# A hybrid encoder layer on eight cores: attention split into producer and consumer pieces, tanh for sigmoid, and a second table started inside the first

## What is computed

```python
h = rms_norm(x, g_mix); q, k, v, x_gate, x_rec = split(h @ w_in)      # 2048 -> 3584
y_attn = windowed_gqa_sink(rope(q), rope(k), v, sink)                # 16 heads of 64, +-128 tokens, sink logit
c = centred_depthwise_conv(x_rec, conv_w, conv_b)                    # 1024 channels
#   rg_lru: r = sigmoid(c @ w_a + b_a); i = sigmoid(c @ w_x + b_x)   # blocks of 64
#           a = exp(-8 r softplus(-lam)); u = sqrt(1 - a*a) * (i * c); h_t = a_t h_{t-1} + u_t
y_lru = gelu(x_gate) * (rg_lru(c, fwd) + rg_lru(c, bwd, reverse=True))
x = x + concat(rms_norm(y_attn), rms_norm(y_lru)) @ w_out
q = rms_norm(x) @ w_pq; s1, s2 = scores of q with 128 + 128 sub-keys per head (8 heads)
gates, eidx = softmax(top 16 of the 16 x 16 best pairs)              # 128 of 16384 experts per token
x = x + sum_e gates_e * gelu(xn . u_emb[e]) * v_emb[e]
out = rms_norm(x, g_final)
```

## Time and profile before

| | us |
|---|---|
| three runs | 6939.51, 6334.04, 7033.96 (median 6939.51) |
| the profiled execution | 6331.23 |
| its span, slowest core (2) | 6329.7 |
| spans of the eight cores | 6294.9 to 6329.7 |
| busy: PE, PEld | 5218.0 (82%), 2522.3 (40%) |
| busy: DVE, ACT, POOL | 3233.7 (51%), 2587.7 (41%), 2413.7 (38%) |

### The profile page before, as it was taken

One profiled execution on the slowest core, in us unless ns is written; L12 is line 12 of the kernel. 1 busy time (PEld: TensorE's weight loads), 2 busy tenths in 40 slices (PEclk: granted clock), 3 DMA queues, 4 the chain that ended last, 5 costly groups with the idle time before them and its releaser, 6 DMA issues.

```text
span 6329.7 us, 87104 instructions; the slowest of 8 cores (6294.9 to 6329.7 us)
## 1 busy us (share of the span) xinstructions
PE 5218.0 (82%) x25339; PEld 2522.3 (40%) x25840; DVE 3233.7 (51%) x6638; ACT 2587.7 (41%) x3722; POOL 2413.7 (38%) x1894
## 2 busy tenths in 40 slices
PE   5895445443687789999999999995799999999994
PEld 2442112111244445555555555442344444444441
DVE  2204556564341876666666666600445555555453
ACT  4523545554222234444444444431344444444443
POOL 1002344344100232222222222300577777777772
PEclk9996566655898999999999999998899999999997
DMA  9731111111973234444444444334554445544542
GB/s 307 236 124 40 41 39 56 43 48 56 268 233 134 80 120 134 146 136 152 137 134 142 139 140 150 128 123 148 181 157 149 152 146 157 157 151 156 155 136 106
DMA packets 388943, 860.25 MB, mean 136 GB/s; under 512 B 95104, under 2 KB 226688, under 8 KB 364928
## 3 DMA queue, kind: packets, MB, share of 16 engines
q1 hardware_dynamic: 374336, 728.82, 37.3%
q0 software_dynamic: 14144, 125.83, 5.0%
HBM read 613.39 MB, written 241.17 MB: 135 GB/s over the span
## 4 chain that ended last, share of the span: by engine, by line
PE 61%; DMA 5%; issue 3%; DVE 3%; ACT 2%; POOL 1%; SPq 1%; DVEq 0%; ACTq 0%; POOLq 0%
PE p_sps L259 28%; PE p_vps L259 25%; PE p_gps L259 4%; PE p_pq L259 2%; DMA s_Gc<-gdn 2%; PE p_pa L259 1%; POOL s_acc L259 1%; PE p_pl L259 1%; SPq L280 1%; DMA s_stfa<-w_out 1%; DMA s_ysqt<-ysq 1%; PE p_psc L259 1%; ACT s_act L259 1%; DVE s_acc L259 1%; DMA gdn<-s_stg 0%
## 5 line engine op out<-in xcount | busy, mean ns | idle before, releaser
L259 PE MATMUL p_sps<-s_xT,s_wq 128*128 128x512 bf16 x7993 | 1822.7, 381 | 28.0 <-ACT s_wq L259 18.3
L259 PE MATMUL p_vps<-s_vr,s_act 128*128 128x512 bf16 x6708 | 1552.7, 383 | 155.2 <-DVE s_acc L259 110.3
L259 POOL TENSOR_TENSOR s_acc<-s_stfa,s_acc 128x512 f32<-128x512 f32 x1024 | 1319.2, 1288 | 501.6 <-ACT s_stfa L259 394.3
L259 PEld LDWEIGHTS p_sps<-s_xT,s_wq 128*128 128x128 bf16 x8192 | 814.8, 100 | 901.1 <-issue 27.1
L259 DVE TENSOR_TENSOR s_acc<-p_vps,s_acc 128x512 f32<-128x512 f32 x1024 | 706.9, 690 | 782.2 <-PE p_vps L259 630.2
L259 PEld LDWEIGHTS p_vps<-s_vr,s_act 128*128 128x128 bf16 x6848 | 673.5, 99 | 981.8 <-issue 194.0
L259 POOL TENSOR_TENSOR s_oA<-s_oA,s_r3T 128x512 bf16<-128x512 bf16 x512 | 552.5, 1081 | 1266.0 <-DVE s_oA L259 1206.1
L259 ACT ACTIVATE s_stfa<-p_vps 128x512 f32<-128x512 f32 x1024 | 556.6, 594 | 951.3 <-POOL s_acc L259 807.7
L259 ACT ACTIVATE s_wq<-p_sps 128x512 bf16<-128x512 f32 x512 | 305.7, 597 | 1102.2 <-PE p_sps L259 1063.0
L259 DVE TENSOR_TENSOR s_oA<-s_iota,s_r3T 128x512 bf16<-128x512 bf16 x512 | 237.0, 463 | 472.1 <-PE p_gps L259 470.0
L259 DVE TENSOR_TENSOR s_act<-s_act,s_Gc 128x1024 bf16<-128x1024 bf16 x256 | 214.6, 838 | 378.9 <-DMA s_Gc<-gdn 378.2
(11 more groups left out here) (164 smaller groups left out, 5242.1 us busy)
## 6 DMA issues: line engine op xcount, KB each, us to landing
s_stfa<-u_t SPq DMA_DIRECT2D x256, 512.0 KB, 4.5
s_stfa<-v_r SPq DMA_DIRECT2D x256, 512.0 KB, 4.7
gdn<-s_stg POOLq DMA_DIRECT2D x32, 2048.0 KB, 8.0
actd<-s_wq SPq DMA_DIRECT2D x128, 512.0 KB, 5.5
s_act<-actd SPq DMA_DIRECT2D x32, 2048.0 KB, 10.0
s_Gc<-gdn SPq DMA_DIRECT2D x128, 512.0 KB, 4.3
s_xt<-x SPq DMA_DIRECT2D x32, 1024.0 KB, 10.7
s_stfa<-w_in SPq DMA_DIRECT2D x52, 512.0 KB, 10.2
```

The costliest lines, as they stand in the source:

```text
L259: pg.op(eng, lambda e: getattr(e, method)(**kw), rd, wr, sig)
```

## The change

Stage B. Every attention piece is cut in two, a half that makes a result (`kvP`, `qP`, `kTP`, `qTP`, `att_vP`, `att_tP`: PE) and a half that reads it (`kvD`, `qD`, ...: DVE and what follows), placed one to three list entries later. The list holds about 280 entries, and `slot()` stands at ten places in a turn, issuing entries in proportion to 266 ticks. `gates` is cut in four quarters. Sigmoid(z) becomes (1 + tanh(z/2))/2, with the halves moved into bias, scale and the products. The banks `pgt` go; gates share three banks `scp` with the scores, `pv` has two. The copy of v goes from ACT to DVE. The memset of `xr` stands before the load.

```diff
@@ stage B
-            scp = [PS(f"scp{i}", [P, 512]) for i in range(2)]
-            pv = PS("pv", [P, 512])
-            pgt = [PS(f"pgt{i}", [P, 512]) for i in range(2)]
+            scp = [PS(f"scp{i}", [P, 512]) for i in range(3)]
+            pvs = [PS(f"pv{i}", [P, 512]) for i in range(2)]
             def load_xr(c, half):
                 if half == 0:
+                    V("memset", [], [xr], ap=xr[:, OWN + 2:OWN + 4], constant=0.0)
                     D("sp", xr[:, 0:OWN + 2], xrT_d[c][:, OWN - 2:SEQ], [xrT_d], [xr])
-                    V("memset", [], [xr], ap=xr[:, OWN + 2:OWN + 4], constant=0.0)
...
+            def kvD(i):
+                p_ = pjm.pop((i, "kv"))
                 rope(p_[:, 0:256], 4, kb[:], p_, kb, i)
-                A("activation", [p_], [va[i % 4]], out=va[i % 4][:, :, 0:64],
-                  in_=p_[:, 256:512].rearrange("p (g d) -> p g d", g=4), func=AF.Copy)
+                V("tensor_copy", [p_], [va[i % 4]], out=va[i % 4][:, :, 0:64], in_=...)
...
+                add(W(kv, kvP, i))
+                add(W(pre, att_n, t - 1))
+                add(W(kv, kvD, i), W(own, qP, i, 0))
+                add(W(pre, att_tP, t - 1))
+                add(W(own, qD, i, 0), W(own, qP, i, 1))
+                add(W(pre, att_tD, t - 1), W(kv, kTP, i))
+                add(W(own, qD, i, 1))
+                add(W(kv, kTD, i), W(att, att_s, t, 0))
+                add(W(att, att_s, t, 1))
+                add(W(own, qTP, i, 0))
+                add(W(att, att_vP, t, 0), W(own, qTD, i, 0))
+                add(W(att, att_s, t, 2), W(own, qTP, i, 1))
+                add(W(att, att_vD, t, 0), W(att, att_vP, t, 1), W(own, qTD, i, 1))
+                add(W(att, att_s, t, 3), W(True, load_ht, i + 2))
+                add(W(att, att_vD, t, 1), W(att, att_vP, t, 2))
+                add(W(att, att_vD, t, 2), W(att, att_vP, t, 3))
+                add(W(att, att_vD, t, 3))
...
+            def gates(n, qd):
+                for tgp in (0, 1) if qd % 2 == 0 else (2, 3):
+                    p_ = scp[nsc[0] % 3]; nsc[0] += 1
                     M([gw[k][c], cb], [p_], out=p_[:], lhsT=gw[k][c][:], rhs=cb[:, sl], start=True, stop=True)
+                    A("activation", [p_, gb], [dstt], out=dstt[:, sl], in_=p_[:], func=AF.Tanh,
+                      bias=gb[:, k * 8 + c:k * 8 + c + 1], scale=0.5)
...
-                V("tensor_tensor", [cc_of(n), ii], [ii], out=ii[:], in0=ii[:], in1=cc_of(n)[:], op=ALU.mult)
+                V("scalar_tensor_tensor", [cc_of(n), ii], [ii], out=ii[:], in0=ii[:], scalar=1.0, in1=cc_of(n)[:], op0=ALU.add, op1=ALU.mult)
...
             for n in range(-2, NU + 1):
+                at(gates, n + 1, 0); at(muls1, n); at(fin_a, n - 1); at(load_xg, n)
+                slot(); at(gates, n + 1, 1); at(muls2, n)
+                slot(); at(gates, n + 1, 2); at(scan, n)
+                slot(); slot(); at(gates, n + 1, 3); at(conv, n + 2, 0)
+                slot(); at(conv, n + 2, 1)
+                slot(); at(fin_b, n - 1, 0)
+                slot(); at(exps, n + 1); at(conv, n + 2, 2)
+                slot(); at(conv, n + 2, 3)
+                slot(); at(fin_b, n - 1, 1); at(conv, n + 2, 4); at(cbcast, n + 2)
+                slot(); at(sqrt_, n + 1); at(fin_g, n)
```

```diff
                     for b in range(NGRP):
                         s_ = sp_[b]
-                        for kc in range(16):
-                            MG([u_, xT[b]], [s_], out=s_[:], lhsT=u_[:, kc * P:(kc + 1) * P], rhs=xT[b][:, kc, :],
-                               start=(kc == 0), stop=(kc == 15))
+                        if b % 2 == 0:
+                            for kc in range(16):
+                                for bb in (b, b + 1):
+                                    MG([u_, xT[bb]], [sp_[bb]], out=sp_[bb][:], lhsT=u_[:, kc * P:(kc + 1) * P], rhs=xT[bb][:, kc, :],
+                                       start=(kc == 0), stop=(kc == 15))
                         A("activation", [s_], [g_], out=g_[:, b * 512:(b + 1) * 512], in_=s_[:], func=AF.Gelu_apprx_tanh)
                         run_bg(share)
-                        if b % 2 == 1:
+                        if b % 2 == 1 and i2 <= P - 4:
                             cv(1, "a")
                     ST("sp", act_d[i2], g_[:], g_, act_d)
-                run_bg(1e9)
+                    if i2 == P - 4:
+                        run_bg(1e9)
+                        ...
+                        for n in range(2):
+                            cv_load(cv_n[0] + n)
+                        load_act(0)
+                        load_G(0, 0)
+                        gate(0, 0)
+                        load_G(0, 1)
+                        gate(0, 1)
+                    if i2 >= P - 4:
+                        cv(2, "ag")
                 pg.barrier()
...
+            for t in range(NT_OWN):
+                D("sp", acc[t][:], x1_d[t][:], [x1_d[t]], [acc[t]])
...
-                    dh, tt = divmod(u, 16) if m + 1 < NCH else divmod(u, 2)[::-1]
+                    dh, tt = divmod(u, 16) if 0 < m < NCH - 1 else divmod(u, 2)[::-1]
...
-                        if u % 4 == 2:
+                        if (u % 2 == 1 if m == 1 and u < 16 else u % 4 == 2 and (m > 0 or u < 16)):
                             cv(1, "a")
```

More of the change, by code:

```diff
@@ L726, in fin_b @@
                     ST("sp", ylT_d[c], ylb[:], ylb, ylT_d)
-            tot = sum(c_ for c_, _ in a1)
-            per = tot / (25.0 * 4)
-            bank = [0.0]
+            NU = len(units)
+            na1 = len(a1)
+            issued = [0]; ticks = [0]
+            NTICK = 25 * 10 + 16
             def slot():
-                bank[0] += per
-                while a1 and bank[0] > 0:
-                    c_, f_ = a1.pop(0)
-                    f_()
-                    bank[0] -= c_
-            NU = len(units)
+                ticks[0] += 1
+                while a1 and issued[0] < na1 * ticks[0] / NTICK:
+                    for f_ in a1.pop(0):
+                        f_()
+                    issued[0] += 1
             def at(f, n, *a):
@@ L749, in build_program @@
                 at(load_xg, n)
[L750 to L753 removed]
                 slot()
+                at(gates, n + 1, 1)
+                at(muls2, n)
+                slot()
+                at(gates, n + 1, 2)
                 at(scan, n)
                 slot()
+                slot()
+                at(gates, n + 1, 3)
                 at(conv, n + 2, 0)
[L758 removed]
                 slot()
                 at(conv, n + 2, 1)
+                slot()
+                at(fin_b, n - 1, 0)
+                slot()
+                at(exps, n + 1)
                 at(conv, n + 2, 2)
+                slot()
+                at(conv, n + 2, 3)
+                slot()
+                at(fin_b, n - 1, 1)
+                at(conv, n + 2, 4)
                 at(cbcast, n + 2)
@@ L773, in build_program @@
                 return nc, pg
+        vst = contextlib.ExitStack()
+        SV, _ = mk(vst)
+        VrW = [SV(f"vrw{i}", [P, DM], BF16) for i in range(5)]
+        actw = SV("actw", [P, 4 * OWN], BF16)
+        gcw = SV("gcw", [P, DM])
         outer = contextlib.ExitStack()
```

188 lines of the change are left out of this document (89 added, 99 removed).

## The result

The changed kernel takes 6152.06 us in the median of four runs (6096.99 to 6481.36), against 6636.77 us for the kernel before in the median of four (6331.72 to 7033.96) on the same chip. Some executions of either kernel are several per cent longer, with one die or both at a lower clock; the ratio of the others is 0.964, with a 95% interval of 0.960 to 0.968. So the change makes the kernel 3.6% faster; the forecast, 6050 of 6331 us, was 4.4%. The profiled execution took 6107.84 us with a span of 6106.3 us (6331.23 and 6329.7 before), inside the range of 5920 to 6200, and 58 us above the forecast of 6050.

What follows compares the result with a forecast made beforehand. PE bounds the first table; in attention no engine is full and the order of waits decides; the seam has idle time. 6331 - 249 (attention) + 15 (first table) - 48 (seam) = 6049, so 6050 us; range 5920 to 6200.

Steps and rivals of the forecast that it cites:

- B, forecast 850: Attention with the recurrence: 762 us of DVE and POOL work, 48 of unit borders, 40 of ends; gain 249 us.
- The signs named for B: Attention stage: 720 to 950 us, DVE waits under 60 us for P*V; POOL over 90% busy would refute.
- I let half of POOL's 288 lie beside it: Attention stage: half of POOL's 288 us overlaps DVE's attention pieces, so 414 + 288 + 204 - 144 = 762 us.
- That nothing would lie beside attention work: Attention stage: DVE and POOL take strict turns, stage 946 us, whole kernel 6145 us; chance 0.17.
- That is all of the 82 us: Attention stage: queuing the memset of xr ahead of its load removes DVE's whole 82 us wait for that load.
- About 56 table loads: ACT in the attention stage: sign that tanh shares exp's table; over 100 loads would mean it does not.
- U, forecast +15: First table, bound by PE: pairing blocks brings one-hot quads two at a time, a 15 us loss, bounds 0 and 54.
- Sharing is worth nothing: First table: one weight tile for two blocks saves no loads; 5 us either way, taken as 0.
- some 1 us per store is left, 15 us: First table: a store lands in about 8 us, a pair of blocks takes 6.9, so ACT's 32 stores lose 15 us.
- rival E: First table: PE waits 1.8 us at each of 256 pairs for a gelu and two evictions, 461 us, total 6495; chance 0.04.
- Hidden by U's matmuls: End of the first table: act, G and v loads, gates and casts moved into its last four tiles cost nothing.
- The seam, forecast -48: Between the tables: acc loads start 49.1 us earlier, less 0.6 for a gelu; gain 48 us, bounds 40 and 55.

## Why the prediction was right or wrong

**B, forecast 850, measured 821 by the windows (gain 270 by one operation, forecast 249): the size was right, its terms were not.** The 850 were 618 us of DVE, 144 that it waits for POOL's turns, 48 of waits at the unit borders and 40 at the ends. Measured, DVE's own operations took 635 us, so the turns lengthened them by 17 and not 144. Between 505 and 1240 us DVE is idle for 136 us (735 less 599 busy), and not 48: P*V 48.0, transposes 28.0, projections 23.5, and only 9.6 for the root, which the 48 were meant for. At the ends it is idle for 50. One term was 127 us too large and another 88 too small, and that they nearly cancel is luck. The signs named for B came true: P*V is at 48 us, under the 60, and POOL is busy 503 of 821 us, 61%, not near the 90% that would have refuted.

**The turns of DVE and POOL.** The step "I let half of POOL's 288 lie beside it" is borne out in size: removing 142 us of it gave 70. It is not borne out as a mechanism, for most of these 70 us were waits (45 of DVE for P*V, which waits for the masks) and only some 14 shorter products and scans. The named sign, "masks on POOL longer in the median than 1.2 us", holds for one mask (2.21) and not for the other (1.15); by the means, 2.33 and 2.10 us (1.78 and 1.72 before), both have grown. The Trainium skill (SBUF — State Buffer, "SBUF: two separate sides") has VectorE or GpSimd wait for the whole instruction of the other at the ports that they share. The trace agrees by the longer operations on both sides, the product's 2.27 us at the shortest and 6.60 at the longest. That nothing would lie beside attention work, which gave 946, is refuted by the 821.

**The memset: half a miss inside a right sum.** "That is all of the 82 us" was read from a row of waits. By itself it was worth 53. The error did not show in the total because the split gave more than was counted for it.

**Tanh.** "About 56 table loads" against 59 measured, and the forecast that tanh shares exp's table is shown by 59 against 131. What the sum did not price is what sigmoid would have cost in the new order, 30 us. The small price of ACT's exponentials was not seen either: their bias is now a tile, 2.10 for 2.00 us, 48 of them, 5 us of ACT.

**U, forecast +15, measured +88 (73 in the median of the cores): the step that failed.** "Sharing is worth nothing" was right: the same 10023 loads, 0.2155 us apart. The step "some 1 us per store is left, 15 us" let the pairing cost nothing but waits behind a store. That term came out near its size: the waits at borders with two quads, most of them behind a store, are 12.4 us with the pairs alone and 19.4 in the changed kernel, and none before. What the sum put at nothing without a reason is the rest. One pair in eight brings three quads or more to two banks, with the gelu of the second block between the evictions: 25 to 27 us of waits for 13.6. And the clock falls behind some of these borders, a cost that no wait shows: with the pairs alone 14 us by the weight loads, up to 20 by the clock records. So the pairing costs 48 us alone and 60 in the changed kernel. That is the kind of loss that rival E names, but at 0.19 to 0.23 us a pair and not 1.8, far from its 1.2 us that turns the sign; the sign "PE shows gaps behind each pair" came true for few of the pairs, and U left its range of 2010 to 2065. The upper bound of 54 counted stores alone and was too narrow for the same reason.

**The moved seam work, the second part of the same miss: "Hidden by U's matmuls" was wrong.** The prediction had named SP's queue and set the waits of act and G loads against the stores of `act_d`. What is behind them and does matter are the loads of v tiles: SP, DVE's gate, SP again, ACT's cast, the gelu, PE. The casts were hidden as work, on an ACT with room, but not as waits. Price: 10 to 21 us, 15 in the median of the cores.

**The seam, forecast -48, measured -45: right**, in the mechanism and nearly in size. The gate of chunk 1 is the last wait, 74 us after the last U matmul, where 75 was forecast. Two small errors cancel in it: the acc loads start 12 us after that matmul and not 4, where the act load stood, and from the first of them to the gate are 62 us and not 68, with fewer v tiles in the queue. How near this stretch is to a bound by transfers (284 GB/s at a share of 0.86 in its first 50 us) the prediction did not say; the two kernels that reordered the loads got 5 and 15 us out of it.

Of the 58 us between forecast and measurement, then, U holds 73, the seam 3 and the stages between 4, and B gives 21 back.

## What to carry to other kernels

A loop that is bound by PE hides small work only in small portions: ask how many bank users come in one bunch, not how much time ACT has on average. Moving work ahead into a busy loop also moves its waits into in-order queues, so walk down each queue (SP's too) for what stands behind a wait on a buffer with one copy. And a row of waits is not what its removal gives: here 53 of 82 us, since the next wait comes earlier. When a forecast comes true, compare its terms too: here two of them were off by 127 and 88 us.

## What the runs showed of the hardware

After a border with five small quads and two waits of 0.35 us in 4 us, TensorE's granted clock fell from 1.00 to 0.57 for the next 4 us and eight matmuls of 512 columns took 0.43 us each; it did so behind six of twelve such borders. The prediction had counted only waits in U. DVE and POOL lengthen each other's operations: the longest product on DVE went from 5.57 to 6.60 us, one mask's median on POOL from 1.15 to 2.21, and taking 142 us of POOL's work away changed that longest product by 0.1 us only. Table loads depend on what ACT does in between: the same 192 gate evictions with sigmoid came with 131 loads in the fine order, against 82 in the coarse one.
